# One Trainium2 core, two transformer blocks: the RWKV core's two pairs on the same rows, a fourth step in its preparation, other banks, rows and order at block 2's first tile, its attention mix and the end

## The reference, cut to what matters

```
block 1: h = rmsnorm(x); u = h @ w_in
  o_b = differential attention (4 heads, two softmaxes each)
  o_a = RWKV-7 time mix (8 heads of 64, a recurrence over the tokens)
  x += (sig(g_a) * (o_a @ w_a) + sig(g_b) * (o_b @ w_b)) @ w_out
  x += relu(rmsnorm(x) @ w_ff1)**2 @ w_ff2
  x += (p @ w_ple) * sig(rmsnorm(x) @ w_ple_gate);  x = rmsnorm(x)
block 2: h = rmsnorm(x); gated linear attention (low-rank input ha = 16 columns of h @ w_in2),
  dilated attention in 3 groups x 4 heads, whose outputs are mixed by a softmax over
  the groups' log-sums; x += mix; x += mlp; x += gate;  y = rmsnorm(x) * ln_f
```

## Time and profile before

| | us |
|---|---|
| median of 3 runs | 2084.71 |
| lowest, highest | 2082.78, 2092.68 |
| the profiled execution: its own time | 2090.74 |
| its span in the profile | 2089.0 |
| PE busy | 2033.5 (97%) |
| DVE, ACT, POOL busy | 983.1 (47%), 775.4 (37%), 278.3 (13%) |
| DMA | 185.47 MB, mean 89 GB/s |

### The profile page before, as it was taken

How to read it: one execution, slowest core, us unless ns; L and a number is a source line. 1 busy time by engine, 2 the same in 40 slices (tenths; PEclk the granted TensorE clock), 3 DMA queues, 4 the chain that set the end, 5 groups by cost and what they waited for, 6 DMA issues and landing times.

```text
span 2089.0 us, 27641 instructions
## 1 busy us (share of the span) xinstructions
PE 2033.5 (97%) x11572; PEld 1631.0 (78%) x11572; DVE 983.1 (47%) x1549; ACT 775.4 (37%) x1233; POOL 278.3 (13%) x279
## 2 busy tenths in 40 slices
PE   8989999999999999999999999999899999999997
PEld 6767677777788778888778888888688888888886
DVE  6655555444553233336754544445643432333365
ACT  5573222123444332234533333334322343322345
POOL 1001221210221000012200000001310120100123
PEclk9999999899999999999999999999999999999999
DMA  5111111111633332222421212222232233223221
GB/s 187 57 65 61 47 47 47 41 47 52 222 101 104 101 106 95 97 100 92 161 71 61 71 61 81 84 79 70 81 101 95 98 117 115 101 91 101 92 95 56
DMA packets 59972, 185.47 MB, mean 89 GB/s; under 512 B 6551, under 2 KB 11799, under 8 KB 59720
## 3 DMA queue, kind: packets, MB, share of 16 engines
q1 hardware_dynamic: 59848, 183.71, 26.0%
HBM read 173.46 MB, written 10.22 MB: 88 GB/s over the span
## 4 chain that ended last, share of the span: by engine, by line
PE 88%; DVE 4%; ACT 4%; issue 2%; POOL 1%; DMA 1%; SPq 0%; DVEq 0%; POOLq 0%; ACTq 0%
PE P L561 25%; PE P L563 24%; PE P L562 24%; DVE AREN L1705 1%; PE P L849 1%; PE P L885 1%; POOL AREN L2425 1%; PE P L939 1%; DVE AREN L1708 1%; PE P L878 1%; PE P L937 1%; PE P L834 1%; ACT WHI L1133 1%; PE P L1062 1%; PE P L1028 1%
## 5 line engine op out<-in xcount | busy, mean ns | idle before, releaser
L561 PE MATMUL P<-HH,WHI 128*128 128x512 f32 x1528 | 623.0, 408 | 10.7 <-DVE HL L1725 3.8
L563 PE MATMUL P<-HH,WLO 128*128 128x512 f32 x1528 | 602.2, 394 | 0.0
L562 PE MATMUL P<-HL,WHI 128*128 128x512 f32 x1528 | 601.7, 394 | 0.0
L1133 ACT ACTIVATE WHI<-RAW 128x1024 fp32r<-128x1024 f32 x302 | 317.9, 1053 | 438.3 <-PE P L563 437.5
L1712 DVE TENSOR_TENSOR WLO<-RAW,WHI 128x1024 fp32r<-128x1024 f32 x302 | 374.8, 1242 | 144.6 <-ACT WHI L1133 143.1
L561 PEld LDWEIGHTS P<-HH,WHI 128*128 128x128 f32 x1528 | 289.9, 190 | 89.0 <-issue 15.9
L561 PE MATMUL P<-ARR,WHI 128*128 128x512 f32 (+1 forms) x920 | 353.8, 385 | 0.0
L563 PE MATMUL P<-ARR,WLO 128*128 128x512 f32 (+1 forms) x920 | 352.9, 384 | 0.0
L562 PE MATMUL P<-ARR,WHI 128*128 128x512 f32 (+1 forms) x920 | 352.8, 383 | 0.0
L563 PEld LDWEIGHTS P<-HH,WLO 128*128 128x128 f32 x1528 | 290.3, 190 | 63.1
L562 PEld LDWEIGHTS P<-HL,WHI 128*128 128x128 f32 x1528 | 290.7, 190 | 55.5 <-issue 0.2
(11 more groups left out here) (304 smaller groups left out, 1555.6 us busy)
## 6 DMA issues: line engine op xcount, KB each, us to landing
RAW<-in_w_in_dram SPq DMA_DIRECT2D x117, 512.0 KB, 3.2
RAW<-in_w_ff_dram SPq DMA_DIRECT2D x64, 512.0 KB, 3.2
RAW<-in_w_ml_dram SPq DMA_DIRECT2D x64, 512.0 KB, 3.2
RAW<-in_w_out_dram SPq DMA_DIRECT2D x16, 512.0 KB, 3.2
RAW<-in_w_pg_dram SPq DMA_DIRECT2D x16, 512.0 KB, 3.2
AREN<-in_xT_dram SPq DMA_DIRECT2D x16, 256.0 KB, 5.7
s_gates<-AREN SPq DMA_DIRECT2D x16, 256.0 KB, 2.0
RAW<-in_w_ab_dram SPq DMA_DIRECT2D x8, 512.0 KB, 3.4
```

Source lines behind the costliest of these rows:

```text
L561: e.matmul(out, hi, H[0][:, s], start=first, stop=False)
L562: e.matmul(out, hi, H[1][:, s], start=False, stop=False)
L563: return e.matmul(out, lo, H[0][:, s], start=False, stop=last)
L1133: e.activation(WHI[n % NSPL][:, :], RAW[n % NRAW][:, :], ACT.Copy).then_inc(*D.act.sig("whi", n))
```

## The change

It only moves work and waits; each product and sum of before is still computed. Attention: heads at rows 39, 65, 91 and 117, the last two steps at 140 and 146, rwkv at rows 149 to 168. Front: four steps a quarter; PE's matmul is in the second, DVE's `max` too, and `k`, `kn` and `ba` are in the third. Its steps stand behind la 3, lb 4, W and N. Both pairs have all their steps on the same rows, from row 212 to 331, and no step of pair 0 is ahead of row 212 any more. Block 2's first tiles: `ha` in bank 4, n4 in bank 5, n5 in bank 6, norm2's steps at `A_EMB2 + 8`, `A_HA + 2` and `A_HA + 7`, and the scaling of `ha` at the second row of `gla`. Mix: seven steps in place of five ahead of the spreading matmuls, which start at row 1558 in place of 1552. End: PE's sum for half 0 comes after the second tile of half 1, ACT's work for it after the last sigmoid, one load of the table; DVE scales tiles 2 to 7 of half 0, POOL tiles 0 and 1.

```
-    for r in (39, 62, 85, 108):
+    for r in (39, 65, 91, 117):
...
-            r + 11, *((r + 12,) if r < 108 else ()), r + 18, r + 18, r + 18, r + 18)
-    put("a", 132, 135)
-    put("r", 117, 119, 119, 122, 122, 125, 125, 128, 128, 131)
-
-    seq = [["f"], ["f"], ["f"]]
+            r + 11, *((r + 13,) if r < 117 else ()), r + 18, r + 18, r + 18, r + 18)
+    put("a", 140, 146)
+    put("r", 149, 153, 153, 156, 156, 160, 160, 164, 164, 168)
+
+    seq = [["f"], ["f"], ["f"], ["f"]]
     for what, q, lev in core_steps():
-        seq.append(["c"] + (["f"] if q < 3 and (what in "WN" or (what, lev) == ("la", 3)) else []))
+        seq.append(["c"] + (["f"] if q < 3 and (what in "WN" or (what, lev) in (("la", 3), ("lb", 4))) else []))
     n = len(seq)
-    late = [A_GA + 4 + i * 121 // n for i in range(n)]
-    early = list(range(A_RW + 68, A_GA + 2, 2))
-    rest = n - len(early)
     for i, group in enumerate(seq):
-        put_at = early[i] if i < len(early) else late[(i - len(early)) * (n - 2) // rest]
-        put_steps(at, put_at, group, 0)
-    for i, group in enumerate(seq):
-        put_steps(at, late[i], group, 1)
-    put("n", A_EMB2 + 14, A_HA + 2, A_HA + 6, *range(A_GL + 1, A_GL + 33, 4))
+        for jj in range(2):
+            put_steps(at, A_GA + 4 + i * 121 // n, group, jj)
+    put("n", A_EMB2 + 8, A_HA + 2, A_HA + 7, *range(A_GL + 1, A_GL + 33, 4))
...
-    put("l", A_HR + 20, A_HR + 20, A_HR + 20, *range(A_HR + 25, A_HR + 50, 6),
-        *[A_HR + r for r in (56, 68, 80, 92) for _ in range(3)], A_HR + 97)
+    put("l", A_HR + 20, A_HR + 20, A_HR + 20, *[A_HR + r for r in (24, 28, 34, 42, 48, 52, 56)],
+        *[A_HR + r for r in (62, 72, 82, 92) for _ in range(3)], A_HR + 98)
...  PE
-                yield from units(("ha",), T_HA, plain(1), H1, hx("HX2"), ev("ha"), (0, 1))
+                yield from units(("ha",), T_HA, plain(1), H1, hx("HX2"), ev("ha"), (4,))
...
-                                if half and t == 5:
+                                if half and t == 6:
                                     last_total(0, 7)
...
             def front(jj):
                 for q in range(4):
+                    yield
                     b = 6 + jj
                     w.wait_ge(F.act.at("sq", q), free.get(b))
...
-                total("n4", 4)
-                yield
-                total("n5", 5)
+                total("n4", 5)
+                yield
+                total("n5", 6)
...
-                for _ in range(5):      (dilated, ahead of the mix's matmuls)
+                for _ in range(7):
...  ACT
-                    if (j, k) == (0, 2):      (high part of ha)
+                    if (j, k) == (0, 4):
...
-                    if (j, k) == (9, 0):
-                        last_rs(0, 7)
...
-                for at in ("sigmoid", "square"):
-                    last_tile(7, 1, at)
+                last_tile(7, 1, "sigmoid")
+                last_rs(0, 7)
+                last_tile(7, 1, "square")
                 last_rs(1, 0)
...
-                    if t == 7:
+                    if t == 7 and half:
                         e.preload_act_table_set("natural_log_exp_and_others")
...  (dilated: exp one step later, the high parts of the weights at the step at row 1548)
+                yield
                 w.wait_ge(L.dve.at("lsub"))
                 e.activation(ar(24, 3)[0:4, :], ar(24, 3)[0:4, :], ACT.Exp).then_inc(*L.act.sig("lex"))
-                for _ in range(3):
+                for _ in range(4):
...  DVE
-                    if k == 7:
-                        w.wait_ge(D.pe.at("ha", 0), M.dve.at("rs"))
-                        mul(HA[0:16, :], bank(0)[0:16, :], RS[0:16, :]).then_inc(*D.dve.sig("ha", 0))
...
-                    if (j, k) == (0, 4):
+                    if (j, k) == (0, 1):
+                        w.wait_ge(D.pe.at("ha", 0), M.dve.at("rs"))
+                        mul(HA[0:16, :], bank(4)[0:16, :], RS[0:16, :]).then_inc(*D.dve.sig("ha", 0))
+                    if (j, k) == (0, 6):
...
-                result(0, 4, 8)
+                result(0, 2, 8)
...
                     e.tensor_scalar(tmp, bank(6 + jj)[:, 0:256], 1e-24, None, op0=ALU.max).then_inc(
                         *F.dve.sig("max", q))
+                    yield
                     w.wait_ge(C.pe.at("t", q - 1, 1), F.pool.at("bh", q - 1, 1), F.dve.at("kp", q))
...  POOL
-                    if (j, k) == (9, 1):
-                        y = v3(ar(8, 8), 8)[:, 0:4, 0:256]
...
+                y = v3(ar(8, 8), 8)[:, 0:2, 0:256]
...  SP
-                parts = ((0, 0, 4, D.pool.at("y")), (0, 4, 8, D.dve.at("y", 0, 8)), (1, 0, 3, D.dve.at("y", 1, 3)),
+                parts = ((0, 2, 8, D.dve.at("y", 0, 8)), (0, 0, 2, D.pool.at("y")), (1, 0, 3, D.dve.at("y", 1, 3)),
```

More of the change, by code:

```diff
@@ L1109, in dilated @@
                     yield
-                for _ in range(5):
+                for _ in range(7):
                     yield
@@ L1268, in dense @@
                     ahead(T_GL, j, k)
-                    if (j, k) == (0, 2):
+                    if (j, k) == (0, 4):
                         w.wait_ge(D.dve.at("ha", 0))
@@ L1550, in norm2 @@
                 w.wait_ge(N.pe.at("sum", "n4"))
-                e.activation(R4, bank(4), ACT.Ln, scale=1.0 / 1024, bias=EPS6).then_inc(*N.act.sig("ln", "n4"))
+                e.activation(R4, bank(5), ACT.Ln, scale=1.0 / 1024, bias=EPS6).then_inc(*N.act.sig("ln", "n4"))
                 w.wait_ge(N.act.at("ln", "n4"))
@@ L2250, in norm2 @@
                 w.wait_ge(M.act.at("r4"), N.pe.at("sum", "n5"))
-                mul(R4, bank(5), R4).then_inc(*M.dve.sig("r4"))
+                mul(R4, bank(6), R4).then_inc(*M.dve.sig("r4"))
                 w.wait_ge(M.act.at("rs"))
@@ L2518, in dense @@
                                 *N.pool.sig("add", "n8", t, half))
-                    if (j, k) == (9, 1):
-                        y = v3(ar(8, 8), 8)[:, 0:4, 0:256]
-                        w.wait_ge(N.act.at("rs", "n8", 0), *[D.act.at("xg", i) for i in range(4)])
-                        mul(y, y, ar(6)[:, 0:256].unsqueeze(1).to_broadcast([128, 4, 256])).then_inc(*D.pool.sig("y"))
                     yield
+                y = v3(ar(8, 8), 8)[:, 0:2, 0:256]
+                w.wait_ge(N.act.at("rs", "n8", 0), *[D.act.at("xg", i) for i in range(2)])
+                mul(y, y, ar(6)[:, 0:256].unsqueeze(1).to_broadcast([128, 2, 256])).then_inc(*D.pool.sig("y"))
             def ya(j):
@@ L2563, in front @@
                     Rq, Kq, _, _, epq, _ = p_.q(q)
-                    yield
-                    yield
+                    for _ in range(3):
+                        yield
                     w.wait_ge(cc(2 * jj), cc(1 + 2 * jj), R.act.at("em", 3), AT.dve.at("ob", 3), C.pe.at("g", q - 1, 1),
@@ L2621, in dilated @@
                         yield
-                for _ in range(8):
+                for _ in range(10):
                     yield
```

## The result

The changed kernel took 2065.19 us (median of 4 executions, 2062.30 to 2069.30), the kernel before 2088.12 beside it (4 executions, 2082.78 to 2092.68); the ratio is 0.9896, 95% interval 0.9873 to 0.9918. Forecast: 2068, "faster" with 0.73. The profiled execution took 2069.3, its span is 2067.5, that is 21.5 us less than before; the forecast was 22.3 less. The sum is right. Its terms are not: errors of 9 to 10 us of either sign cancel, which is luck. The largest lesson is that the core's joint rows, a main part of the change, cost time beside four front steps.

What follows compares the result with a forecast made beforehand. PE's work bounds the kernel (busy 2033.5 of 2089.0 us), so gains come from idle time or the higher clock. Terms sum to -22.3 us, giving 2068; its own range is 2062 to 2075 (55%), the wider one 2056 to 2083.

Steps and rivals of the forecast that it cites:

- Attention and rwkv: Attention's end: PE's waits for rwkv's tanh and the last head's square go, with low clock behind them; -7.1 us (-5 to -8).
- The later front steps: Core, line 781: six waits for ACT's square go with the sum one step later; -8.1 us (-7 to -8.1).
- the first joint front: Start of the core, both pairs' first front: some 4 us idle, about as before; 0 us (-2 to +3).
- The rest of the joint core: Core: both pairs' answers come in one bunch to DVE, ACT and POOL, mostly covered; +1 us (-3 to +10).
- The clock in the core: Core: a clock fall at each of four joint steps O, 43 us low in place of 33; +4.7 us (-16 to +14).
- Rival 1: Core: joint steps stall, PE waiting 0.42 us for DVE in all 66 steps, 28 us; 2096 us, chance 5%.
- Rival 3: Core: clock falls follow waits, not step O; the core loses 16 us less; 2048 us, chance 5%.
- Rival 2: Core: low clock stretches of 17 us four times, 68 us in place of 33, eat the gain; 2082 us, chance 15%.
- Block 2's first tiles: Block 2's start: the bank waits ahead of ha and gla go, and the low clock too; -8.2 us (-4 to -9.5).
- The mix: Mix: PE's 5.66 us wait for the split weights falls to 2.9, with half the clock's cost; -4.5 us (0 to -9).
- From there the same steps as before, spread over one more row each: Mix, after tile 3 at about 1448: unchanged steps put the first weights at about 1468.8, PE at 1466.
- The end: Kernel's end: output DMAs take the place of the chain as the limit; -0.1 us (-1 to +1.5).

Runs made afterwards that it cites:

- one row behind: The changed kernel with every step of pair 1 one row behind the same step of pair 0; 2080.85 us, ratio 0.9977.
- eight groups behind: The changed kernel with pair 1 eight groups of steps behind pair 0, both still from row 212 to 331; 2051.53 us, ratio 0.9840.
- `hr` on DVE: The changed kernel with the product of gate and tile in hr on DVE in place of POOL; 2057.34 us, ratio 0.9867.
- the combination that holds: Changed kernel, pair 1 eight groups behind, hr's product on DVE, mix's seventh step at row 1548, DVE doing half 0 in three pieces; 2046.99 us, ratio 0.9796.
- four front steps alone: The kernel before with the front in four steps, the pairs on their old rows; 2071.73 us, ratio 0.9915.
- joint rows alone: The kernel before with both pairs on the same rows from row 212 on and three front steps a quarter; 2086.14 us, ratio 0.9998.
- three groups behind: The changed kernel with pair 1 three groups of steps behind pair 0; 2058.90 us, ratio 0.9855.
- the banks alone: The kernel before with only block 2's first-tile banks changed (ha 4, n4 5, n5 6), rows unchanged; 2085.99 us, ratio 0.9992.

## Why the prediction was right in sum and wrong in its terms

**Attention and rwkv (-7.1; measured -3.3).** By the marks it is 5.1, but 1.8 of that is the first front's wait. Both waits of the earlier trace rows went, 5.3 us. The step that failed is "The wider spacing of the heads only adds cover": two new waits came, 2.05 us, since the heads' step for pt now falls on another row of a tile. DVE stands at the low part (waiting for ACT's high part) with the softmax behind it, and a fall of the clock behind the waits took back the clock's share. DVE first, then PE:

```profile
110.00 1.22 DVE L1709 TENSOR_TENSOR WLO<-RAW,WHI 128x1024 fp32r<-128x1024 f32 x1 [3.31 <-ACT WHI L1129]
```

```profile
114.81 0.87 PE L738 MATMUL P<-CST,AREN 128*128 128x128 f32 x6 [1.08 <-DVE AREN L2117]
116.65 1.12 PE L738 MATMUL P<-CST,AREN 128*128 128x128 f32 x4 [0.97 <-ACT AREN L1420]
117.42 0.78 PE L556 MATMUL P<-HH,WHI 128*128 128x512 f32 x1
117.99 0.63 PE L557 MATMUL P<-HL,WHI 128*128 128x512 f32 x1
```

In four of the seven profiles with the same rows here (one row behind, eight groups behind, `hr` on DVE, the combination that holds) that fall did not come: rows 40 to 164 took 131.0 us in place of 132.6, with the two waits still there. So of the part's gain 1.6 us depends on the execution.

**The later front steps (-8.1) and the first joint front (0).** Right. The six later waits went, 8.1 us. At the front's start PE waited 1.13 + 0.43 + 0.76 + 1.92 = 4.24 us where I had 4:

```profile
208.75 0.70 PE L777 MATMUL P<-AREN,CST 128*128 128x256 f32 x2 [1.13 <-ACT AREN L1478]
209.88 0.70 PE L777 MATMUL P<-AREN,CST 128*128 128x256 f32 x2 [0.43 <-ACT AREN L1478]
214.78 1.71 PE L830 MATMUL P<-AREN 64*128 64x128 f32 x16 [0.76 <-DVE AREN L1702]
218.41 2.58 PE L830 MATMUL P<-AREN 64*128 64x128 f32 x16 [1.92 <-POOL AREN L2425]
```

**The rest of the joint core (+1; measured -2.4).** New are 2.3 us at line 881, twice 1.16; gone are seven small waits of before, 4.7 us, which the prediction did not count. So the sign was wrong, within the range. Rival 1 is out. (`core_steps` lists 70 steps, not 66, which makes rival 1's 28 us 29.)

**The clock in the core (+4.7; measured about +7).** The mechanism was right: a fall came in each of the four joint steps O, and one more behind the waits of the first front. Its length was not: 54.6 us in place of 43 (6.8 at the front, then 6.8, 17.1, 13.7 and 10.2, where I had 12, 12, 12 and 6.9). Its price was not either: the core loses 0.35 us per us (the fit below) where I took 0.47, so 20.5 us more cost 7.1. The fall comes in the middle of the joint step, with PE busy ahead of it, and a pair of small matmuls goes from 0.25 us (415.67 to 415.92) to 0.40 (417.36 to 417.76):

```profile
415.67 0.32 PE L933 MATMUL P<-AREN 64*64 64x64 f32 x2
415.92 0.33 PE L935 MATMUL P<-AREN 128*64 128x64 f32 x2
...
416.95 0.48 PE L935 MATMUL P<-AREN 128*64 128x64 f32 x2
417.36 0.47 PE L933 MATMUL P<-AREN 64*64 64x64 f32 x2
417.76 0.47 PE L935 MATMUL P<-AREN 128*64 128x64 f32 x2
```

That also prices it: 0.15 / 0.40 = 0.37 us lost per us at the lower level, where a dense row loses 0.47. Rival 3, the clock that minds idle time alone, is out: waits fell by 8 us and the low time grew by 20. So the rule of the Trainium skill weighed in the prediction ("TensorE: Matmul & The Clock Gate", "What's actually happening") does not agree with these rows: PE's records are busy up to the fall. Other falls of these traces do follow waits: in the mix 10 us at the lower level stood behind the wait of 5.43 us, and with the wait gone (the combination that holds) none came. So waits are one thing that the falls follow here, and long steps of small matmuls another.

**What I left out: switches.** Each time PE goes from dense rows to small matmuls and back, the matmuls at the seam start later. In the core's timelines a dense matmul within dense work starts 0.23 us behind the last, one at a seam 0.32 or 0.34. A seam is counted where a dense matmul follows a small one. Before has 93 seams, the changed kernel 71. Over twelve profiled cores (8 arrangements) a fit by least squares of the core's time less its waits gives 280.7 us + 0.285 a seam + 0.347 per us of low clock, with no core off by more than 2.2 us (a fit prices the seam; no run changes seams alone):

```
core (rows 164-332)       us    waits  seams  low clock us   fit
before                   335.4   14.8    93      34.1       333.8
changed                  326.0    6.6    71      54.6       326.4
four front steps alone   317.1    3.6    93      20.5       317.9
joint rows alone         327.6   13.0    71      41.0       328.1
one row behind           341.0    5.3   117      64.9       341.8
eight groups behind      312.7    4.4    79      17.1       313.5
three groups behind      323.0    4.8    74      41.0       320.8
```

By it the change gave 8.2 in waits and 6.3 in seams and lost 7.1 to the clock: 7.4 of the 9.4 measured between the marks. So the step of the prediction that failed in the core is the list of what joint rows change: it had waits and the clock, not the seams (6.3 us), and it left out the small waits that went. Rival 2, the clock eating the gain, was half true: against four front steps alone the joint rows cost 8.9 us, by the fit 34.1 us more of low clock (11.8) less 22 seams (6.3) plus 3.0 of waits, 8.5. That the steps are joint by pairs is the cause and not the later start alone: with a lag of eight groups the start is as late and the core takes 312.7.

**Block 2's first tiles (-8.2; measured -8.7).** Right step by step: 1.65 us at n4 and 0.42 at n5 (forecast 1.6 and 0.6), no low clock, and none in any of the eight profiles with these rows. The clock's share is partly luck of the profile of before: against the kernel with joint rows alone the same rows gained 5.6 us, not 8.7. Banks and rows were both needed: the banks alone took 2.1 of the 7.1 us of rows 1056 to 1080, since DVE's five sums from 1033.00 on the earlier trace rows set n4.

**The mix (-4.5; measured -0.6).** The step that failed is "From there the same steps as before, spread over one more row each". The first half was right: tile 3 was read 7.93 us behind tile 2 (forecast 8). DVE after that, changed kernel:

```profile
1419.46 0.69 DVE L1702 TENSOR_TENSOR AREN<-P,RS 128x512 f32<-128x512 f32 x1 [0.66 <-PE P L558]
...
1427.39 0.68 DVE L1702 TENSOR_TENSOR AREN<-P,RS 128x512 f32<-128x512 f32 x1
...
1435.54 0.68 DVE L1702 TENSOR_TENSOR AREN<-P,RS 128x512 f32<-128x512 f32 x1
...
1442.26 0.68 DVE L1702 TENSOR_TENSOR AREN<-P,RS 128x512 f32<-128x512 f32 x1
...
1449.37 0.68 DVE L1702 TENSOR_TENSOR AREN<-P,RS 128x512 f32<-128x512 f32 x1
1449.97 2.97 DVE L2396 TENSOR_TENSOR ARR<-AREN,ARR 4x512 fp32r<-4x512 f32 x3
```

PE waits for that last split:

```profile
1450.70 2.07 PE L1112 MATMUL P<-ARR,EYE 4*128 4x512 f32 x4 [5.43 <-DVE ARR L2396]
```

Two things. The last step had moved past the reading of one more tile (row 1551), so a whole round through DVE, ACT, POOL and ACT stood ahead of it, 7.1 us here, which took back what exp's new place had given; the kernel with that one row moved back shows it. And a round takes 6.7 to 8.2 us in place of the 5.4 that PE needs for 8 rows (before: 5.4, 6.8 and 6.8), in part since POOL and DVE hold each other. Counted from the reading of tile 2, the last split began 30.5 us later in the changed kernel and 26.7 us later before: 5.9 less up to tile 3, 2.7 more over the next two rounds, 7.1 more for the extra one. PE comes six rows, 4.1 us, later, so the wait hardly moved, 5.43 in place of 5.66 us. The forecast's clock share was also mis-sized: half of what 10.2 us at the lower level cost is 2.4 us, not 1.5. The holding of POOL and DVE:

```profile
1421.18 1.43 POOL L2425 TENSOR_TENSOR AREN<-AREN 128x512 f32<-128x512 f32 x1 [6.71 <-ACT AREN L1279]
1429.65 3.72 POOL L2425 TENSOR_TENSOR AREN<-AREN 128x512 f32<-128x512 f32 x1 [7.04 <-ACT AREN L1279]
1436.97 3.13 POOL L2425 TENSOR_TENSOR AREN<-AREN 128x512 f32<-128x512 f32 x1 [3.59 <-ACT AREN L1279]
```

```profile
1421.49 2.73 DVE L2377 TENSOR_TENSOR AREN<-AREN 4x1536 f32<-4x1536 f32 x1
...
1429.41 1.74 DVE L2388 RECIPROCAL AREN<-AREN 4x256 f32<-4x256 f32 x1
1431.08 1.15 DVE L1709 TENSOR_TENSOR WLO<-RAW,WHI 128x1024 fp32r<-128x1024 f32 x1
...
1436.14 1.73 DVE L2388 RECIPROCAL AREN<-AREN 4x256 f32<-4x256 f32 x1
1437.80 1.15 DVE L1709 TENSOR_TENSOR WLO<-RAW,WHI 128x1024 fp32r<-128x1024 f32 x1
```

The product begun at 1429.65 ends at 1433.37, 1.14 us behind the end of DVE's low part (1432.23); the next ends at 1440.10, 1.15 behind (1438.95). At 1421.18 POOL was first, and DVE's difference took 2.73 us in place of the 1.75 of before. That agrees with the exclusive lock that the Trainium skill describes in "SBUF — State Buffer", section "SBUF: two separate sides". With the product on DVE the wait was 2.24 us shorter, so the lock is part of the lateness and DVE's own list the rest. I had it in the prediction for the end and not here, where it mattered.

**The end (-0.1; measured -0.3).** Right: PE's rows gave 2.9 us and the output took back 2.6. The data run without a gap at some 340 GB/s for 6.2 us:

```profile
2061.00:2063.00 2.00, 0.00 (x0) 0.00 (x0) 1.71 (x3) 0.00 (x0) 0.00 (x0) 0.50 1.03 342
2063.00:2065.00 2.00, 0.00 (x0) 0.00 (x0) 0.00 (x0) 0.00 (x0) 0.00 (x0) 0.50 1.03 340
```

POOL's two tiles took 2.83 us, begun beside DVE's first product and ending 1.12 us behind it (2060.42, 2059.30), so they waited for each other here too; the data hid it. With the DMAs as the limit only an earlier first piece helps, and a piece of two tiles gave 1 us.

**Not forecast: the merge (+2.5).** PE waited 2.33 us for a low part at 521.95 (1.76 before) with 3.4 us of low clock behind it. In the changed kernel ACT stands there at a sigmoid whose input comes by DMA, with the high part queued behind. Rows 332 to 400 have the same steps in all twelve kernels and took 46.94 to 50.91 us (changed: 50.80, before: 48.29). The stretch varies between executions; what sets it was not tested.

## What to carry to other kernels

Before merging two streams onto the same rows, list what each long step without dense work does to the clock, and put the long steps of one against the short ones of the other: the same steps on the same rows with a shift of eight groups were worth 14 us. When a step is moved by a few rows, look not at the rows but at what it passes in each engine's list; one tile's reading passed is a whole round through four engines, 7.1 us here. And when a term of a sum is "fewer waits", test that part alone: here one edit gave 16 us, and by the profiles of the two kernels the one beside it took 9 back in the core.

## What the runs showed of the hardware

- The difference between executions of one kernel goes with the clock. 41 executions of the kernel before lie between 2079.47 us at a mean clock of 0.991 and 2093.74 at 0.983; a line through them falls 1.6 us per 0.001. 0.001 of 2089 us is 4.2 us at the lower level, so 0.38 us per us, which agrees with the fit's 0.35.
- A product of POOL begun 0.24 us into a reciprocal of DVE with a single input (1429.65) ended only 1.14 us behind the low part that followed, 3.72 us in all, where the same product takes 1.29 us with DVE idle (1407.91). Whether it is the reciprocal or the low part queued right behind it that holds POOL first is not separated by these runs.
